# A three-block transformer kernel on one core: reordered steps in the convolution stage and in cross attention

## The chip, the core and the metric

The program runs on one core of a Trainium2 chip. The metric is the device time of one execution in microseconds (us); shown are the median of three runs and one profiled execution. TensorE is called PE here, VectorE DVE, ScalarE ACT, GpSimd POOL and SyncE SP, as in the profile.

## What is computed

512 tokens of width 1024 in float32 go through a first network (two layers of mixer, MLP and gated embedding) and then a second block, to which the change is confined:

```python
def second_block(x, mem, positions, ...):
    h = h + hybrid_mixer(rmsnorm(h), ...)      # w_in, w_out
    h = h + cross_attention(rmsnorm(h), rmsnorm(mem), w_cq, w_ckv, w_co)
    h = h + conv_ffn(rmsnorm(h), w_up, ffn_dw_w, w_down)
    return rmsnorm(h)

def hybrid_mixer(...):
    # q, k, v: 4 heads; q and k in two halves of 64, partly rotated
    a = softmax(q0 k0) - lam * softmax(q1 k1)     # causal, per head
    a = rmsnorm(a @ v) * 0.8
    c = u1 * sigmoid(u2)
    c = silu(layernorm(causal_dwconv(c, 31 taps)))   # 512 channels
    return concat(a, c) @ w_out

def cross_attention(h, m, ...):
    # 4 heads of 256, 256 memory tokens
    p = softmax(q @ k / 16);  return (p @ v) @ w_co
```

## The kernel before, in words

Activations lie features first: 8 tiles of 128 features by 512 tokens. Every product in float32 is made of three passes of a reduced format: a tensor is split into a high part (`aH`, written by ACT) and the rest (`aL`, written by DVE), weights likewise (`wH`, `wL`), and PE sums high by high, low by high and high by low (lines 468 to 470). One `linear` is 8 feature tiles times 3 passes, 24 matmuls of 512 columns.

**Weights.** SP copies pieces of 128x512 numbers in the order of `PLAN` into 4 buffers `raw`; POOL splits each into one of 7 pairs `wH`, `wL` (lines 2557 and 2559), and may write a pair only when PE has released the piece 7 back. A linear consumes 2 pieces. `open3` (plan) and `three_open`, `three_step` (PE) run three linears side by side, one feature tile after the other.

**Order.** Nothing schedules: each engine has its own function (`pe`, `act`, `dve`, `pool`, `sync`) in which the work is written in the order of issue, and an engine waits in that order for events of the others (`wait_ge`, `then_inc`). PE takes PSUM banks from a queue of 8 with `take`; `give(b, V, "rL", j)` puts a bank back and names the event that frees it, so a later, unrelated step can wait for that event.

**Convolution stage** (w_in to w_out). For each of the 4 heads of differential attention: `rotary_in(j)` is the linear of queries or keys, ACT copies it to `tmp[j % 2]`, `rotate(j)` is one PE permutation of `tmp`, three DVE steps turn it and `rotated(j)` splits it into `d_qH`, `d_qL`, `d_kH`, `d_kL`. `d_scores(hd)` are the scores in four row blocks n (line 978), with softmax by DVE (maxima, line 2359) and ACT (exponentials, line 1206). `d_turned(hd)` transposes the probabilities (line 1007) and splits them into `uH`, `uL`. `d_values(hd)` multiplies by the values. `stat_end("dn", hd)` sums the squares (line 501), ACT makes the root (`rstd`), `d_normed(hd)` normalizes and splits. The convolution's 31 taps run on DVE for three groups of 128 channels (`some_taps`) and on PE for the fourth, as diagonal matrices that ACT makes (`diagonals`, `conv_taps`, line 996). The layer norm takes its mean by PE ("mu", line 1051), squares on ACT, their sum on DVE and PE. `memory_keys` and `xvalues(half)` are keys and values of the memory for cross attention.

**Cross attention.** `stat_end("z")` and `columns("z")` turn the norm of the queries into a column; `x_head_in(hd)` are the two linears of a head's queries, `x_scores`, `x_turned` (line 1114), `x_values` the attention, and eight linears of `w_co` follow. `stat_end("f")` sums the squares for the next norm.

The lines that set the order in the convolution stage, on PE:

```python
for hd in range(2):
    d_turned(hd)
    d_scores(hd + 1, {1: conv_taps, 2: rotary_in(2 * hd + 4)})
    rotary_in(2 * hd + 5)
    rotate(2 * hd + 4); rotate(2 * hd + 5)
    conv_taps(20 + 8 * hd, min(24 + 8 * hd, 31))
    d_values(hd)
    stat_end("dn", hd, tiles=1, tail=False)
```

Of the kernel before, what the change touches and what calls it, by code (L numbers as in the profile page):

```python
# [37 lines left out]
def plan():  # L38
# [121 lines left out]
    for o in range(8):  # L160
        tile8("w_co_2", 0, 128 * o)
# [118 lines left out]
BY_PE = 3  # L280


def build(nc, xT, pT, memT, pos, pos2, vec, cst, ws, out):
    PLAN, BEHIND, DIVIDED = plan()
    with ExitStack() as ctx:
# [147 lines left out]
        def pe():  # L433
# [3 lines left out]
            def take(*event):  # L437
# [106 lines left out]
            def three_step(lin, k, xH, xL, ready, first=0, last=7, only=None):  # L544
                ws_, bs, events = lin
                for i in range(3):
                    if only in (None, i):
# [3 lines left out]
                        j = three(bs[i].ap[:, :], H, L, xH[:, k, :], xL[:, k, :], k == first, k == last)  # L551
# [406 lines left out]
            def rotate(j):  # L958
                b = take("rts", j)
# [51 lines left out]
            def d_values(hd):  # L1011
# [9 lines left out]
                give(b, V, "y2L", hd)  # L1021
# [17 lines left out]
            for hd in range(2):  # L1039
# [52 lines left out]
            def x_head_in(hd):  # L1092
                for d in range(2):
                    linear(("xq", hd, d), (V, "xqL", hd, d), "w_cq_2", 0, 128 * (2 * hd + d), aH, aL, z_ready)
# [36 lines left out]
            x_head_in(0)  # L1131
            x_scores(0)
            for hd in range(4):
                if hd < 3:
                    x_head_in(hd + 1)
                else:
                    P.also("z done")
                x_turned(hd)
                if hd < 3:
                    x_scores(hd + 1)  # L1140
                x_values(hd)
            P.also("x heads done")
            for o in range(8):
                w = block("w_co_2", 0, K8, ((128 * o, 128),))
                b = take("co", o)
                for k, (H, L, c, end) in enumerate(w):
                    P.wait_ge(G, "w", c)
                    P.wait_ge(V, "xoL", k // 2, k % 2)
# [6 lines left out]
            stat_end("f")  # L1155
            P.also("end cross")
            P.wait_ge(A, "end cross")
            P.wait_ge(V, "end cross")
# [23 lines left out]
        def root(*sid):  # L1182

            if sid[0] in ("mix", "mlp", "ple", "hs", "cq", "ckv", "ln"):
                return bk("stat", *sid)[:, :]
            return tab[1][0][:, 0:256] if sid == ("mem",) else rs[:, :]
# [3 lines left out]
        def act():  # L1190
# [397 lines left out]
            def rotary_in(j):  # L1588
                A.wait_ge(P, "rt", j)
                if j > 1:  # L1590
# [9 lines left out]
            def d_scores(hd):  # L1600
# [5 lines left out]
                for n in range(4):  # L1606
# [9 lines left out]
                    if n:  # L1616
                        divide(n - 1)
                divide(3)
# [13 lines left out]
            def d_normed(hd):  # L1632
                A.wait_ge(V, "dn", hd)
                do(uH[:, hd, :], bk("do", hd)[:, :], ACT.Copy).then_inc(*A.did("y2H", hd))
# [23 lines left out]
            d_scores(0)  # L1658
            diagonals(12, 16)
            rotary_in(2)  # L1660
# [4 lines left out]
            for hd in range(2):  # L1665
                d_turned(hd)
                d_scores(hd + 1)
                diagonals(20 + 8 * hd, 28 + 8 * hd)
                rotary_in(2 * hd + 4)
# [6 lines left out]
            convolved(2)  # L1676
            for i in range(4):
# [1016 lines left out]
```

## Time and profile before

| what | value |
|---|---|
| median of 3 runs (lowest, highest) | 2405.92 us (2403.82, 2407.05) |
| profiled execution, its own time | 2401.89 us |
| its span, first to last instruction | 2400.0 us |
| PE busy | 2298.3 us, 96% |
| POOL busy | 1563.6 us, 65% |
| DVE busy | 1269.0 us, 53% |
| ACT busy | 648.8 us, 27% |
| mean granted TensorE clock | 0.988 |

The profile counts an engine busy from the start of an instruction to its end; PE's ends are modelled and overlap the next start. Times in rows of the trace are us from the start of the span. The granted clock is 1.00 at 2.4 GHz and 0.50 at 1.2 GHz. The convolution stage ends near 1862 us; cross attention runs from there to 2028 us.

### The profile page before, as it was taken

To read this page: it belongs to the slowest core of one execution; us is meant where nothing else is said; L and a number is where in the kernel's file an instruction comes from. 1 tells how busy PE (TensorE), PEld (TensorE's weight loads), DVE (VectorE), ACT (ScalarE), POOL (GpSimd) and SP (SyncE) were. 2 spreads that over 40 slices of the span, in tenths; PEclk is the share of its full clock that TensorE was granted. 3 is DMA by queue.
4 is the path that set the end of the run, shared out by engine and by line. 5 is a ranking of instruction groups with operands and counts; after the bars stand their busy time and mean duration, and the time that the engine had idled before them with its cause. 6 is when DMAs were issued, how large, how long until landed. Compare 5 with 4: busy or idle time off the path is not lost.

```text
span 2400.0 us, 27442 instructions
## 1 busy us (share of the span) xinstructions
PE 2298.3 (96%) x10372; PEld 1860.2 (78%) x10372; DVE 1269.0 (53%) x1820; ACT 648.8 (27%) x1190; POOL 1563.6 (65%) x1530
## 2 busy tenths in 40 slices
PE   8999989999998899999999999999988999999998
PEld 6888877888887577778778888778647787888886
DVE  6674726235346666165454364468763443635444
ACT  3443432101014355154221011141444232202112
POOL 7556557877775454554597777598315946878784
PEclk9999999999999899999999999999998999999999
DMA  5222222333332111211233333233112422333332
GB/s 163 77 71 82 68 80 83 107 99 98 97 92 75 53 39 37 70 40 45 75 117 105 99 110 101 79 101 106 48 31 71 113 63 79 97 98 96 99 95 75
DMA packets 110867, 200.13 MB, mean 83 GB/s; under 512 B 12304, under 2 KB 18704, under 8 KB 110736
## 3 DMA queue, kind: packets, MB, share of 16 engines
q1 hardware_dynamic: 107568, 194.72, 27.0%
q10 hardware_dynamic: 3168, 3.67, 0.5%
q8 instruction: 82, 1.34, 0.2%
q14 instruction: 49, 0.40, 0.0%
HBM read 196.24 MB, written 2.10 MB: 83 GB/s over the span
## 4 chain that ended last, share of the span: by engine, by line
PE 87%; DVE 7%; ACT 2%; POOL 2%; issue 1%; DMA 0%; SPq 0%; DVEq 0%; POOLq 0%; ACTq 0%
PE bank L468 26%; PE bank L470 26%; PE bank L469 26%; DVE bank L1801 2%; DVE h L1793 1%; POOL wL L2559 1%; PE bank L501 1%; PE bank L996 1%; POOL wH L2557 1%; PE bank L862 1%; PE bank L867 1%; PE bank L868 1%; PE bank L863 1%; PE bank L864 1%; DVE aL L1801 1%
## 5 line engine op out<-in xcount | busy, mean ns | idle before, releaser
L2559 POOL TENSOR_TENSOR wL<-raw,wH 128x512 fp32r<-128x512 f32 (+2 forms) x731 | 997.9, 1365 | 60.9
L2557 POOL TENSOR_SCALAR wH<-raw 128x512 fp32r<-128x512 f32 (+2 forms) x731 | 528.9, 724 | 650.3 <-PE bank L470 558.4
L468 PE MATMUL bank<-aH,wH 128*128 128x512 f32 x1376 | 546.1, 397 | 18.1 <-DVE aL L1801 8.8
L470 PE MATMUL bank<-aH,wL 128*128 128x512 f32 x1376 | 537.6, 391 | 0.0
L469 PE MATMUL bank<-aL,wH 128*128 128x512 f32 x1376 | 537.1, 390 | 0.0
L468 PE MATMUL bank<-uH,wH 128*128 128x512 f32 x960 | 375.5, 391 | 5.6 <-DVE uL L1793 5.6
L469 PE MATMUL bank<-uL,wH 128*128 128x512 f32 x960 | 374.4, 390 | 0.0
L470 PE MATMUL bank<-uH,wL 128*128 128x512 f32 x960 | 374.3, 390 | 0.0
L468 PEld LDWEIGHTS bank<-aH,wH 128*128 128x128 f32 x1376 | 258.8, 188 | 77.8 <-issue 12.4
L469 PEld LDWEIGHTS bank<-aL,wH 128*128 128x128 f32 x1376 | 259.0, 188 | 56.3 <-issue 3.7
L470 PEld LDWEIGHTS bank<-aH,wL 128*128 128x128 f32 x1376 | 258.7, 188 | 54.9
L468 PEld LDWEIGHTS bank<-uH,wH 128*128 128x128 f32 x960 | 180.8, 188 | 44.6 <-ACT uH L1205 6.4
L469 PEld LDWEIGHTS bank<-uL,wH 128*128 128x128 f32 x960 | 180.8, 188 | 37.9 <-issue 0.5
L470 PEld LDWEIGHTS bank<-uH,wL 128*128 128x128 f32 x960 | 180.7, 188 | 37.8
L1205 ACT ACTIVATE uH<-mr 128x512 fp32r<-128x512 f32 x64 | 40.5, 633 | 391.0 <-DVE mr L1801 391.0
L1793 DVE TENSOR_TENSOR F<-F,bank 128x512 f32<-128x512 f32 x56 | 38.5, 687 | 190.0 <-PE bank L470 190.0
L1801 DVE SCALAR_TENSOR_TENSOR mr<-bank,rs 128x512 f32<-128x512 f32 x64 | 44.0, 688 | 157.9 <-PE bank L470 142.0
L1801 DVE SCALAR_TENSOR_TENSOR bank<-F,vs,bank 128x512 f32<-128x512 f32 x138 | 103.8, 752 | 34.9 <-ACT bank L1205 23.8
L1793 DVE TENSOR_TENSOR h<-h,bank 128x512 f32<-128x512 f32 x88 | 60.4, 686 | 112.4 <-PE bank L470 110.8
L1793 DVE TENSOR_TENSOR sums<-sums,sq 128x512 f32<-128x512 f32 (+1 forms) x72 | 78.3, 1088 | 76.5 <-ACT sq L1205 76.4
L2566 POOL TENSOR_SCALAR m_P<-m_P,m_stat 128x512 f32<-128x512 f32 x64 | 44.7, 698 | 102.0 <-DVE m_stat L2217 100.0
L1801 DVE SCALAR_TENSOR_TENSOR c_cb<-c_xb,vs,c_cb 128x511 f32<-128x511 f32 x88 | 82.4, 937 | 40.3 <-ACT c_cb L1205 38.7
(306 smaller groups left out, 3209.7 us busy)
## 6 DMA issues: line engine op xcount, KB each, us to landing
raw<-in_ws SPq DMA_DIRECT2D x699, 256.0 KB, 2.6
raw<-in_ws SPq DMA_DIRECT2D x24, 192.0 KB, 2.3
h<-in_xT SPq DMA_DIRECT2D x4, 512.0 KB, 6.6
E<-in_memT ACTq DMA_DIRECT2D x16, 128.0 KB, 2.5
out<-c_F SPq DMA_DIRECT2D x8, 256.0 KB, 2.1
tmp<-in_pT ACTq DMA_DIRECT2D x4, 256.0 KB, 3.6
raw<-in_ws SPq DMA_DIRECT2D x8, 128.0 KB, 2.0
g_hc<-in_cst SPq DMA_DIRECT2D x1, 640.0 KB, 9.2
```

Of the source, the lines that this page charges most:

```text
L468: P.e.matmul(o, lH, rH, start=start, stop=False, skip_group_check=skip)
L469: P.e.matmul(o, lH, rL, start=False, stop=False, skip_group_check=skip)
L470: return P.e.matmul(o, lL, rH, start=False, stop=stop, skip_group_check=skip)
L501: i = P.e.matmul(b.ap[:, 0:n], ones, sums[:, 0:n], start=True, stop=not tail)
L862: P.e.matmul(b.ap[:, :], m_qnH[:, c], m_knH[:, :], start=True, stop=False)
L863: P.e.matmul(b.ap[:, :], m_qnH[:, c], m_knL[:, :], start=False, stop=False)
L1205: return A.e.activation(o, i, func, bias=bias, scale=scale)
L1793: return V.e.tensor_tensor(o, a, b, op)
L1801: return V.e.scalar_tensor_tensor(o, a, s, b, op0, op1)
L2557: G.e.tensor_scalar(H, x, 1.0, 0.0, MUL, ADD).then_inc(*G.did("wH", n))
L2559: G.e.tensor_tensor(L, x, H.bitcast(F32), SUB).then_inc(*G.did("w", n))
L2566: G.e.tensor_scalar(x, x, m_st[:, 4 * (hd % 2) + n, 2:3], 0.0, MUL, ADD).then_inc(*G.did("mP", hd, n))
```

## The change

PE, ACT and DVE are given another order from the first rotated head to the first linear of the last feed-forward. No multiplication is added or removed; a DVE sum of four squares is written as a tree, and three results get another place (`tmp[0]` for the normalized head, `C` for the layer norm's root, `C` and `Sn` for squares). `order` lists instructions as they are issued. Names: `tmp` the copied projection, `F` the diagonals and probabilities, `cs` constants, `d_VH` values, `x_kH` memory keys; line numbers of the changed kernel are larger.

PE, head 1 of the convolution stage, from the last matmul of its second projection (before; the values follow both permutations and the taps):

```order
L470 MATMUL bank<-aH,wL 128x512
L961 MATMUL bank<-tmp,cs 128x512 x2
L996 MATMUL bank<-F,sq 128x512 x4
L468 MATMUL bank<-uH,d_VH 128x512
L469 MATMUL bank<-uL,d_VH 128x512
```

and from the last matmul of the values to the next scores:

```order
L470 MATMUL bank<-uH,d_VL 128x128
L501 MATMUL bank<-sums,cs 128x512
L1007 MATMUL bank<-cs,F 128x128 x10
L978 MATMUL bank<-d_kH,d_qH 128x128 x2
L978 MATMUL bank<-d_kL,d_qH 128x128 x2
```

The changed order at the same two places:

```order
L471 MATMUL bank<-aH,wL 128x512
L963 MATMUL bank<-tmp,cs 128x512
L469 MATMUL bank<-uH,d_VH 128x512
L470 MATMUL bank<-uL,d_VH 128x512
L471 MATMUL bank<-uH,d_VL 128x512
```

```order
L471 MATMUL bank<-uH,d_VL 128x128
L963 MATMUL bank<-tmp,cs 128x512
L998 MATMUL bank<-F,sq 128x512 x3
L502 MATMUL bank<-sums,cs 128x512
L998 MATMUL bank<-F,sq 128x512
L1009 MATMUL bank<-cs,F 128x128 x10
```

The values now stand between the two permutations, and the second permutation and three taps between the values and the sum of squares, one tap behind it.

ACT at the end of the first head's softmax, before:

```order
L1206 ACTIVATE bank,d_stat<-bank,d_stat 128x512 [waits dve_tile_written]
L1205 ACTIVATE F<-F,d_stat 128x384 [waits dve_tile_written]
L1205 ACTIVATE F<-F,d_stat 128x512 [waits dve_tile_written]
L1205 ACTIVATE sq<-cs,vs 128x128 [waits pe_group_done] x4
L1205 ACTIVATE tmp<-bank 128x512 [waits pe_group_done] x2
```

and in the change:

```order
L1230 ACTIVATE F<-F,d_stat 128x256 [waits dve_tile_written]
L1230 ACTIVATE sq<-cs,vs 128x128 [waits pe_group_done] x4
L1230 ACTIVATE tmp<-bank 128x512 [waits pe_group_done]
L1231 ACTIVATE F,d_stat<-bank,d_stat 128x512 [waits dve_tile_written]
L1231 ACTIVATE bank,d_stat<-bank,d_stat 128x512 [waits dve_tile_written]
L1230 ACTIVATE F<-F,d_stat 128x384 [waits dve_tile_written]
L1230 ACTIVATE F<-F,d_stat 128x512 [waits dve_tile_written]
```

The four diagonals and the first copy to `tmp` moved ahead of the last row block's exponentials.

PE in cross attention around the transposes of a head, before:

```order
L469 MATMUL bank<-aL,wH 128x512
L470 MATMUL bank<-aH,wL 128x512
L1114 MATMUL bank<-cs,F 128x128 x8
L468 MATMUL bank<-x_kH,uH 128x256
L469 MATMUL bank<-x_kL,uH 128x256
```

and in the change:

```order
L470 MATMUL bank<-aL,wH 128x512
L471 MATMUL bank<-aH,wL 128x512
L1120 MATMUL bank<-cs,F 128x128 x8
L469 MATMUL bank<-aH,wH 128x512
L470 MATMUL bank<-aL,wH 128x512
```

One of the two query linears now stands behind the transposes, ahead of the next scores. The diff, cut to its core:

```diff
@@ plan
-    for o in range(8):
+    open3(*[("w_co_2", 0, 128 * o) for o in range(3)])
+    for o in range(3, 8):
         tile8("w_co_2", 0, 128 * o)
@@ pe: take, rotate, d_values
-                b = banks.pop(0)
+                b = banks.pop(1 if second else 0)
...
-                give(b, V, "y2L", hd)
+                give(b, V, "dn", hd)
@@ pe: heads 0 and 1 of the convolution stage
-                rotate(2 * hd + 5)
-                conv_taps(20 + 8 * hd, min(24 + 8 * hd, 31))
                 d_values(hd)
+                rotate(2 * hd + 5, second=True)
+                conv_taps(20 + 8 * hd, 23 + 8 * hd)
                 stat_end("dn", hd, tiles=1, tail=False)
+                if hd == 0:
+                    conv_taps(23, 24)
+            d_turned(2)
             b = take("mu")
...
-            d_turned(2)
             d_scores(3, {1: lambda: memory_keys(4)})
             memory_keys(6)
-            stat_end("ln", tiles=4, tail=False, freed=(V, "lnn", 3))
+            b = take("stat", "ln")
+            P.wait_ge(V, "sum", ("ln",))
+            P.e.matmul(b.ap[:, :], ones, sq[:, :], start=True, stop=True).then_inc(*P.did("stat", "ln"))
+            give(b, A, "ln", "ln")
             d_values(2)
+            d_turned(3)
             stat_end("dn", 2, tiles=1, tail=False)
-            d_turned(3)
             xvalues(0)
             d_values(3)
-            stat_end("dn", 3, tiles=1, tail=False)
...
                 three_step(lin, k, uH, uL, y2_ready, last=3)
+                if k == 0:
+                    stat_end("dn", 3, tiles=1, tail=False)
@@ pe: cross attention
-            stat_end("z")
             xvalues(1)
-            columns("z")
+            stat_end("z")
...
+            def co_step(*ks):
+                for k in ks:
+                    three_step(lin, k, None, None, co_ready, tiles=x_o)
...
-            x_head_in(0)
+            x_head_in(0, 0)
+            columns("z")
+            x_head_in(0, 1)
+            x_head_in(1, 0)
             x_scores(0)
             for hd in range(4):
                 if hd < 3:
-                    x_head_in(hd + 1)
+                    x_head_in(hd + 1, 1)
+                x_turned(hd)
+                if hd < 2:
+                    x_head_in(hd + 2, 0)
+                elif hd == 2:
+                    lin = three_open([("w_co_2", 0, 128 * o) for o in range(3)], [("co", o) for o in range(3)])
+                    co_step(0)
                 else:
-                x_turned(hd)
+                    co_step(2, 3)
                 if hd < 3:
                     x_scores(hd + 1)
+                if hd == 2:
+                    co_step(1)
                 x_values(hd)
-            for o in range(8):
+            co_step(4, 5, 6, 7)
+            for o in range(3, 8):
...
-            stat_end("f")
...
                         linear(("cu", tile, j), ...)
+                        if tile == 0 and j == 0:
+                            stat_end("f")
@@ act
-            diagonals(12, 16)
-            rotary_in(2)
+            d_scores(0, {2: lambda: (diagonals(12, 16), rotary_in(2))})
...
+                d_scores(hd + 1, {2: lambda: (convolved(2) if hd else None, diagonals(20 + 8 * hd, 28 + 8 * hd), rotary_in(2 * hd + 4))})
                 rotary_in(2 * hd + 5)
                 rotate(2 * hd + 4)
+                d_values(hd)
                 rotate(2 * hd + 5)
-                d_values(hd)
                 rstd(128, "dn", hd)
+                d_turned(hd + 1)
                 d_normed(hd)
...
+            d_scores(3, {1: squares})
             memory_keys(4)
             memory_keys(6)
+            d_values(2)
             rstd(512, "ln")
+            d_turned(3)
             rstd(128, "dn", 2)
...
+            xvalues(1)
             rstd(1024, "z")
@@ dve
+            d_scores(0, {2: lambda: some_taps(4)})
+            turned_by_cos(2)
             rotate(2)
+            turned_by_cos(3)
             rotate(3)
...
+                d_scores(hd + 1, {2: lambda: some_taps(4)} if hd == 0 else {1: lambda: some_taps(200)})
+                turned_by_cos(2 * hd + 4)
+                some_taps(1)
                 rotate(2 * hd + 4)
+                turned_by_cos(2 * hd + 5)
+                rotated(2 * hd + 4)
                 rotate(2 * hd + 5)
                 rotated(2 * hd + 5)
                 d_normed(hd)
+                d_turned(hd + 1)
```

`turned_by_cos` is the first of the three DVE steps of a rotation, now issued by itself; `between` runs a function after row block n. `d_normed` writes `tmp[0]`, so its bank is freed by the first step of the norm ("dn") and no longer by the last ("y2L").

## Rows read from the trace of the kernel before

**Rows 1.** The page, part 1: busy us, share of the span, instructions.

```profile
PE 2298.3 (96%) x10372; PEld 1860.2 (78%) x10372; DVE 1269.0 (53%) x1820; ACT 648.8 (27%) x1190; POOL 1563.6 (65%) x1530
```

**Rows 2.** Windows: stretch, length, busy PE, PEld, DVE, ACT, POOL, granted clock, DMA.

```profile
1762.00:1766.00 4.00, 4.00 (x8) 1.70 (x8) 3.17 (x8) 2.06 (x9) 0.00 (x0) 0.57 0.02 4
...
1799.00:1807.00 8.00, 4.96 (x25) 4.96 (x26) 4.77 (x13) 4.21 (x15) 1.78 (x2) 0.57 0.01 3
...
1827.00:1834.00 7.00, 5.14 (x13) 4.07 (x14) 3.36 (x7) 3.52 (x5) 1.90 (x2) 0.51 0.01 2
...
1905.00:2030.00 125.00, 119.26 (x573) 97.85 (x573) 53.86 (x115) 35.26 (x75) 71.14 (x73) 1.00 0.27 80
```

**Rows 3.** PE's waits, 1717 to 1863 us: for whom, us in total, times, longest.

```profile
PE bank L468 <- DVE F L1801: 5.2, 1, 5.2
PE bank L978 <- DVE uL L1793: 3.3, 3, 2.6
PE bank L468 <- DVE uL L1793: 3.1, 1, 3.1
PE bank L501 <- ACT sums L1205: 2.9, 4, 0.8
PE bank L961 <- ACT tmp L1205: 2.3, 3, 1.7
PE bank L468 <- DVE d_qL L1793: 2.2, 2, 1.6
PE bank L1051 <- ACT F L1205: 1.6, 1, 1.6
PE bank L978 <- DVE F L1801: 0.6, 1, 0.6
```

**Rows 4.** PE's waits, 1863 to 2035 us.

```profile
PE bank L468 <- DVE uL L1793: 4.5, 5, 1.4
PE bank L504 <- ACT sq L1205: 2.4, 2, 1.2
```

**Rows 5.** Timeline of PE at the z norm: start, us, instruction, idle before.

```profile
1889.45 0.40 PE L470 MATMUL bank<-uH,wL 128*128 128x512 f32 x1
1889.68 1.02 PE L501 MATMUL bank<-sums,cs 128*128 128x512 f32 x2
```

**Rows 6.** Timeline of PE, a matmul of `xvalues(0)` at the lower clock.

```profile
1831.56 0.63 PE L468 MATMUL bank<-wH,x_mH 128*128 128x512 f32 x1
```

**Rows 7.** Timelines of PE, ACT and DVE from head 0's sum of squares.

```profile
1755.27 1.13 PE L501 MATMUL bank<-sums,cs 128*128 128x512 f32 x2 [0.69 <-ACT sums L1205]
1756.23 1.25 PE L1007 MATMUL bank<-cs,F 128*128 128x128 f32 x10
...
1761.21 0.39 PE L978 MATMUL bank<-d_kH,d_qH 64*128 64x256 f32 x2 [0.23 <-DVE uL L1793]
...
1758.61 1.91 ACT L1205 ACTIVATE uH<-bank 128x512 fp32r<-128x512 f32 x5 [0.83 <-DVE bank L1801]
...
1757.82 0.76 DVE L1801 SCALAR_TENSOR_TENSOR bank<-bank,lam,rs 128x512 f32<-128x512 f32 x1 [4.16 <-ACT rs L1205]
1759.31 2.28 DVE L1793 TENSOR_TENSOR uL<-bank,uH 128x512 fp32r<-128x512 f32 x5 [0.73 <-ACT uH L1205]
```

**Rows 8.** Timelines of POOL and DVE before and in `xvalues(1)`.

```profile
1886.00 1.82 POOL L2559 TENSOR_TENSOR wL<-raw,wH 128x512 fp32r<-128x512 f32 x1
...
1897.20 1.30 POOL L2559 TENSOR_TENSOR wL<-raw,wH 128x512 fp32r<-128x512 f32 x1
...
1899.16 1.29 POOL L2559 TENSOR_TENSOR wL<-raw,wH 128x512 fp32r<-128x512 f32 x1
...
1886.59 1.78 DVE L1793 TENSOR_TENSOR sums<-sums,sq 128x512 f32<-128x512 f32 x1
```

**Rows 9.** Timelines: first scores of cross attention (PE), last division (DVE).

```profile
1917.73 0.39 PE L468 MATMUL bank<-x_kH,uH 128*128 128x256 f32 x1 [1.41 <-DVE uL L1793]
...
1923.69 0.81 DVE L1797 TENSOR_SCALAR F<-F,x_stat 128x256 f32<-128x256 f32 x1
```

More of the change, by code:

```diff
@@ L435, in pe, with take @@
             at = 0
-            def take(*event):
-                b = banks.pop(0)
+            def take(*event, second=False):
+                b = banks.pop(1 if second else 0)
                 if b.freed:
@@ L542, in three_done, with three_step @@
                     j.then_inc(*P.did("w", lin[0][i][k][2]))
-            def three_step(lin, k, xH, xL, ready, first=0, last=7, only=None):
+            def three_step(lin, k, xH, xL, ready, first=0, last=7, only=None, tiles=None):
                 ws_, bs, events = lin
@@ L550, in three_step @@
                         ready(k)
-                        j = three(bs[i].ap[:, :], H, L, xH[:, k, :], xL[:, k, :], k == first, k == last)
+                        x = tiles[k] if tiles else (xH[:, k, :], xL[:, k, :])
+                        j = three(bs[i].ap[:, :], H, L, *x, k == first, k == last)
                         three_done(lin, i, k, j, last)
@@ L956, in rotary_in, with rotate @@
                 linear(("rt", j), (V, "rL", j), "w_in_2", 0, (512 if j % 2 else 0) + 128 * (j // 2), aH, aL, n1_ready)
-            def rotate(j):
-                b = take("rts", j)
+            def rotate(j, second=False):
+                b = take("rts", j, second=second)
                 P.wait_ge(A, "rt", j)
@@ L1086, in pe, with x_head_in @@
             P.also("y2 done")
[L1087 removed]
             xvalues(1)
             P.also("mem done")
[L1090 to L1094 removed]
+            stat_end("z")
+            def x_head_in(hd, d):
+                linear(("xq", hd, d), (V, "xqL", hd, d), "w_cq_2", 0, 128 * (2 * hd + d), aH, aL, z_ready)
             def x_scores(hd):
@@ L1617, in d_scores @@
                         divide(n - 1)
+                    if n in between:
+                        between[n]()
                 divide(3)
@@ L1633, in d_normed @@
                 A.wait_ge(V, "dn", hd)
-                do(uH[:, hd, :], bk("do", hd)[:, :], ACT.Copy).then_inc(*A.did("y2H", hd))
+                do(uH[:, hd, :], tmp[0][:, :], ACT.Copy).then_inc(*A.did("y2H", hd))
             def convolved(i):
@@ L1718, in act, with x_head_in @@
             A.wait_ge(P, "y2 done")
+            xvalues(1)
             rstd(1024, "z")
-            xvalues(1)
-            def x_head_in(hd):
-                for d in range(2):
-                    A.wait_ge(P, "xq", hd, d)
-                    if hd > 1:
-                        A.wait_ge(P, "xs", hd - 2, 3)
-                    do(x_qH[hd % 2][:, d, :], bk("xq", hd, d)[:, :], ACT.Copy).then_inc(*A.did("xqH", hd, d))
+            def x_head_in(hd, d):
+                A.wait_ge(P, "xq", hd, d)
+                if hd > 1:
+                    A.wait_ge(P, "xs", hd - 2, 3)
+                do(x_qH[hd % 2][:, d, :], bk("xq", hd, d)[:, :], ACT.Copy).then_inc(*A.did("xqH", hd, d))
             def x_scores(hd):
@@ L2363, in d_scores @@
                         combine(n - 1)
+                    if n in between:
+                        between[n]()
                 combine(3)
@@ L2372, in d_normed @@
             def d_normed(hd):
-                y = bk("do", hd)[:, :]
+                y = tmp[0][:, :]
                 V.wait_ge(A, "rstd", "dn", hd)
-                stt(y, y, lam[:, 5:6], root("dn", hd), MUL, MUL).then_inc(*V.did("dn", hd))
+                V.wait_ge(V, *(("rr", 2 * hd + 4) if hd < 2 else ("y2L", hd - 1)))
+                stt(y, bk("do", hd)[:, :], lam[:, 5:6], root("dn", hd), MUL, MUL).then_inc(*V.did("dn", hd))
                 V.wait_ge(V, "dn", hd)
@@ L2419, in dve, with add_ln_squares @@
                 stt(d_acc[:, i, :], bk("mu")[:, :], -1.0 / 512, d_acc[:, i, :], MUL, ADD).then_inc(*V.did("cent", i))
-            for i in range(1, 4):
-                add_squares(("ln",), i)
-            d_turned(2)
-            d_scores(3)
+            def add_ln_squares():
+                x = (sq, tmp[1], C, Sn)
+                for i in (0, 2):
+                    V.wait_ge(A, "sq", ("ln",), i + 1)
+                    tt(x[i][:, :], x[i][:, :], x[i + 1][:, :], ADD).then_inc(*V.did("sum2", ("ln",), i))
+                V.wait_ge(V, "sum2", ("ln",), 2)
+                tt(sq[:, :], sq[:, :], C[:, :], ADD).then_inc(*V.did("sum", ("ln",)))
+            d_scores(3, {1: add_ln_squares})
             memory_keys(4)
             memory_keys(6)
-            d_normed(2)
             V.wait_ge(A, "rstd", "ln")
@@ L2457, in dve, with x_head_in @@
             residual("z", "wo", ("z",), lambda k: vv("norm_cross_g_2", k))
+            def x_head_in(hd, d):
+                V.wait_ge(A, "xqH", hd, d)
+                low(x_qL[hd % 2][:, d, :], bk("xq", hd, d)[:, :], x_qH[hd % 2][:, d, :]).then_inc(*V.did("xqL", hd, d))
             xvalues(1)
+            x_head_in(0, 0)
             column(x_rc[:, 0, :], "z")
@@ L2462, in dve @@
             ts(x_rc[:, 2, :], x_rc[:, 0, :], -1.0 / 16, None, MUL, None).then_inc(*V.did("xrc"))
-            def x_head_in(hd):
-                for d in range(2):
-                    V.wait_ge(A, "xqH", hd, d)
-                    low(x_qL[hd % 2][:, d, :], bk("xq", hd, d)[:, :], x_qH[hd % 2][:, d, :]).then_inc(*V.did("xqL", hd, d))
             def x_scores(hd):
```

81 lines of the change are left out of this document (41 added, 40 removed).

## The prediction

> **What bounds the kernel now.** I read the page's line of busy engines first [rows 1]: PE is busy 2298.3 us of a span of 2400.0, the next engine, POOL, 65%. PE works in the order in which its instructions are written, so the time is PE's work plus PE's waits plus what the clock takes. Then came the view of waits, for PE alone, over the two stages that the change touches. In the convolution stage PE waits 21.2 us in 16 waits [rows 3], in cross attention 6.9 us in 7 [rows 4]; together 28.1 us in 23. Then the timelines around each wait, to find the step that ends late and what stands next on PE. Last the windows with the granted clock [rows 2]: three stretches, of 4, 8 and 7 us, show 0.57, 0.57 and 0.51, which is 1.2 GHz nearly throughout, while the stretch of 125 us in cross attention shows 1.00. In all three, PE had waited several times between short matmuls before the clock fell.
>
> A wait costs more than its idle time. A matmul that follows another at once starts 0.23 us behind it, one that follows a wait needs 0.40 us from start to end [rows 5]: about 0.16 us of refill for each wait.
>
> PE's work does not change: the diff moves matmuls and removes none. The gain can come from three places only: idle time, refill, clock. I add them up, and then look at what the moved steps hide behind.
>
> **The change, part by part.**
>
> *The waits of the convolution stage.* The largest, 5.2 us, is the first matmul of `xvalues(0)`, which waits for a bank that the layer norm's last scaling frees. Its new place follows values, transposes and the sum of squares, and the norm starts earlier: it goes. The 3.1 us (a `memory_keys` bank) and the 2.2 us of the values' bank were waits for lows that an unrelated step releases; another place in the queue of banks or an earlier release ("dn" in place of "y2L") removes them. The 2.9 us in 4 before the sums of squares are DVE and ACT turning the values into squares with nothing on PE meanwhile; now a permutation and taps or another head's transposes stand there, each about 1 us. The 2.3 us in 3 before the permutation (line 961) vanish since the copy to `tmp` is issued by ACT ahead of the last exponentials and the second permutation stands behind the values. The 1.6 us before the mean have the transposes of head 2 in front.
>
> What stays, or is new, I work out one by one:
> - (a) The 0.6 us before the scores that depends on DVE's probabilities: nothing near it moves. 0.5 us.
> - (b) Head 0's last group of transposes now needs the bank that the norm's first step frees. Before, from the start of the sum of squares to the end of that step took 1757.82 + 0.76 − 1755.27 = 3.3 us [rows 7]. PE has meanwhile the sum of squares (0.96 us, from 1755.27 to 1756.23), a tap of the same form (taken as 0.96 too) and nine of the ten transposes (1.0 of 1.25 us, less the refill): 2.9 us. 0.4 to 0.5 remain.
> - (c) The next scores, row block 1, need a bank freed by the lows of the transposed probabilities. These now stand behind the norm: 3.3 us to the norm, one ACT step more in between (estimated at 0.6, from five uH copies of mixed width in 1.91 us), 0.7 to the first lows, and 1.9 from these to the scores (1759.31 to 1761.21, [rows 7]): 6.5 us from the start of the sum. PE is there at 3.4 + 0.9 = 4.4. A wait of 2.1 us, in place of the 2.6 of [rows 3].
> - (d) Head 1 as (b), but with no tap behind its sum: 3.3 − 1.9 = 1.4 us.
> - (e) Some short waits of the transposes of head 3 for banks, 0.3 us together.
>
> Together 4.8 us of 21.2 in the convolution stage.
>
> *Cross attention.* The three waits of about 0.6 us and the one of 1.4 us in [rows 4] were values behind transposes whose lows were not yet there; a whole linear (24 matmuls of 0.23, 5.5 us) or a step of three output linears (2.1 us) stands between now. They go; (g) that of the last head, about 1.2 us, stays. The 2.4 us of the two sums of squares go: the first now stands behind `xvalues(1)`, the second behind the first linear of the next stage. But `xvalues(1)` then starts at 1889.7 where the sum stood [rows 5] and no longer behind it and its wait, and eats pieces faster than POOL makes them: 6 matmuls, 1.4 us a piece, against 1.96 us for a pair (1897.20 to 1899.16, from low part to low part [rows 8]). Its eighth piece is wanted at 1889.7 + 7 × 1.4 = 1899.5 and ready at 1899.16 + 1.29 = 1900.45: (f) a wait of 1.0 us.
>
> Is the softmax still covered, with one linear of queries there where two stood? In [rows 9] the last division ends at 1923.69 + 0.81 = 1924.5, 6.8 us after the first of the scores. Scores are 24 matmuls of half the columns, 2.9 us, and the linear is 5.5: 8.4 us. It is, with 1.6 us to spare. Were it not, each head would pay the lack at once, on PE.
>
> Sum of the waits: 28.1 − 4.8 − 1.0 − 1.2 = 21.1 us gone. Some ten waits remain of 23; 13 × 0.16 = 2.1 us of refill.
>
> *Clock.* A granted clock of 0.57 means 0.50 for 86% of the stretch. PE was busy in the three stretches 4.00, 4.96 and 5.14 us [rows 2], of which at the lower level about 3.4 + 4.3 + 5.1 = 12.8 us, and a matmul of 512 columns took 0.63 us there [rows 6] against 0.40. Half of this busy time is the loss, 6.4 us. The longest waits of the pattern go, but (b) with (c), and (d), are still waits among small matmuls, so I keep two stretches of the kind of the first, 3.4 us each, PE busy throughout: 3.4 us of loss. Gain 3.0. The ends are no gain (or a loss of 3, if each of the two lasts as long as the second did) and 6.4.
>
> *At nothing.* DVE's and ACT's instructions keep their number and engines at 53% and 27% [rows 1]; the moved taps and diagonals go where these engines waited (DVE 4.16 us ahead of the norm's step [rows 7]). If that cover were gone, the norm chain of (b) to (d) would grow by as much. Three output linears opened early hold six weight pairs of the 7 at most for a step of 2.1 us each; POOL then has its work later, not more. The step of the residual, three tiles at once, is caught up by the fifth output tile.
>
> **Sum.** 21.1 + 2.1 + 3.0 = 26.2 us against the profiled execution's 2401.89, which lies 4.0 under the median of the runs; the same difference from the median gives 2405.9 − 26.2 = **2379.7 us**.
>
> **The rivals.**
>
> *The clock stays low as long as before.* For it: the waits (b) to (d) still alternate with short matmuls, as in [rows 2]. Against: the summed idle time in that stage falls to a quarter. The time: gain 23.2, 2382.7 us. Chance 0.15. By the Trainium skill, TensorE: Matmul & The Clock Gate, section "A second HAM failure mode: psum-queue depth-cycling", short idle times between groups of matmuls are enough to make the clock swing, so on that page's rule alone this rival would be the forecast; the trace agrees that the clock fell among such waits.
>
> *POOL becomes the bound in `xvalues(1)`.* With DVE's sum of 1.78 us beside it, the low part took 1.82 instead of 1.29 [rows 8]. If the pairs came every 2.4 us in the place of 1.96, the wait (f) would be 1.0 + 8 × 0.4 = 4 to 5 us: 2384 us. Chance 0.08. The Trainium skill, GPSIMD Engine Reference, section "1. Specifications", has GpSimd's SBUF interfaces shared with VectorE, with contention where a DVE instruction has two SBUF inputs; both long rows are of that kind.
>
> *New waits behind the moved steps take half.* Each bank freed by an earlier event puts a later, unrelated step behind it; (b), (c) and (d) could be 3 us each if ACT or DVE, with the steps of the softmax interleaved, comes to the norm later than before. Then half of the gain remains: 2393 us. Chance 0.12.
>
> *Slower: the clock falls in cross attention.* There it is 1.00 over 125 us, because long linears stand between the groups of short matmuls; the change leaves one linear where two stood. If it fell there, a microsecond of work at half the clock costs another: from 26 us of full-speed work done at 1.2 GHz, a fifth of that stretch, the whole gain is lost; with three fifths of it, 75 us, the sum is 2379.7 + 75 = 2455 us. Against: the waits there shrink too, to 2.2 us. Chance 0.03.
>
> *No difference.* The rest, 0.02: the order on PE does change, as its listing shows, so this needs two mishaps at once.
>
> **The numbers.** The forecast as worked out has 0.60. Its own bounds: if (b) to (f) all vanish, 5 us better, and with the whole clock back 3.4 more, 2371; if (f) is 4, (c) and (d) twice as long and the clock gives nothing, 10 worse, 2390. Both at their ends is unlikely. The range that holds 8 in 10 is 2373 to 2391.5; outside lie most of "half is taken" and the slow case, and the best corner. A measurement of this kernel tells 0.2%, 4.8 us, from no change: faster 0.94, same 0.03 and slower 0.03, since every case but the last two is faster by 12 us or more.
>
> **What would show it.** In the profile after, PE's busy time should lie 3 us lower or so, and its waits between the heads' first rotation and the output projection should sum to about 5 us, not 21, with none above 2.5; no wait at the first matmul of `xvalues(0)` or at the permutations; in cross attention one of about 1.2 in the last values, and one of about 1 in `xvalues(1)` that names POOL's wL. The windows should show at most two short stretches near 0.5, and 1.00 through the heads of cross attention. Wrong I would be if waits for the norm's banks, "dn" or the low parts, stand there with several us each, if POOL's wait in `xvalues(1)` is over 3, or if the clock falls in a new place.

## The result

The changed kernel took 2371.48 us (median of 4 runs, 2370.67 to 2372.49), the kernel before 2406.34 us beside it (4 runs, 2403.82 to 2407.05): ratio 0.9857, 95% interval 0.984 to 0.9874, 34.9 us faster. The forecast was 2379.7 us, 26.2 us faster, with a range down to 2373: the direction was right and the gain a quarter too small, 1.5 us outside the range.

| what | before | after |
|---|---|---|
| profiled execution, its own time | 2401.89 us | 2372.49 us |
| its span | 2400.0 us | 2370.6 us |
| PE's waits, convolution stage | 21.2 us in 16 | 4.2 us in 4 |
| PE's waits, cross attention | 6.9 us in 7 | 0.6 us in 2 |
| stretches near 1.2 GHz in the changed part | 3 | none |

The page of the changed kernel, part 1, in the order of [rows 1]:

```profile
PE 2291.2 (97%) x10372; PEld 1857.8 (78%) x10372; DVE 1271.2 (54%) x1820; ACT 648.5 (27%) x1190; POOL 1568.0 (66%) x1530
```

The numbers of instructions are those of before, on every engine: nothing was added or left out. PE is 7 us less busy for the same 10372 matmuls, which is the clock and the refills of all stages together.

PE's waits of the changed kernel, 1717 to 1842 us, to be read against [rows 3] (engine, tile, line, releaser: us in total, times, longest):

```profile
PE bank L980 <- DVE uL L1826: 2.6, 2, 2.0
PE bank L1009 <- DVE tmp L1834: 1.6, 2, 1.2
```

and 1842 to 2010 us, against [rows 4]:

```profile
PE bank L469 <- POOL wL L2612: 0.6, 2, 0.3
```

Seven of the eight groups of [rows 3] have vanished. What is left are the scores behind the lows of the transposed probabilities (0.6 and 2.0) and, new, the transposes behind the norm's first step (0.4 and 1.2), both of which the prediction named. In cross attention only POOL's weights in `xvalues(1)` are waited for.

Windows of the changed kernel (stretch, length, busy PE, PEld, DVE, ACT, POOL, granted clock, DMA), against [rows 2]:

```profile
1754.00:1764.00 10.00, 7.62 (x38) 4.24 (x38) 7.27 (x17) 5.54 (x16) 0.00 (x0) 1.00 0.01 2
1784.00:1790.00 6.00, 4.76 (x19) 2.40 (x17) 3.37 (x7) 3.25 (x7) 0.00 (x0) 1.00 0.00 1
1795.00:1842.00 47.00, 47.00 (x254) 39.17 (x254) 21.80 (x38) 23.38 (x45) 34.18 (x34) 1.00 0.30 90
1842.00:2010.00 168.00, 167.40 (x788) 137.19 (x787) 79.31 (x139) 47.30 (x95) 119.55 (x116) 1.00 0.31 91
```

The first two hold the waits that remain, and the clock stays at 2.4 GHz through both. Where before three stretches of 19 us in all lay mostly at 1.2 GHz, none does.

**The changed part by itself.** The two kernels issue the same PE instructions up to the last group of eight taps ahead of the change (the row `L996 MATMUL bank<-F ... x8`, L998 in the changed kernel), and again at the end. So one window from that row to 339 us before the last instruction holds the same 1526 matmuls in every kernel of this document. Before, and in the change:

```profile
1700.34:2060.95 360.61, 332.30 (x1526) 256.44 (x1526) 179.85 (x333) 122.30 (x269) 191.53 (x190) 0.98 0.23 69
1704.15:2031.59 327.44, 322.61 (x1526) 252.12 (x1526) 183.18 (x333) 121.99 (x269) 196.41 (x190) 1.00 0.26 76
```

The changed part is 33.2 us shorter: PE is busy for 9.7 us less and idle for 23.5 us less. The whole profiled executions differ by 29.4 us only, because the 7404 matmuls ahead of this window, the same in both kernels, are done by 1700.3 us in one execution and by 1704.2 in the other.

### The profile page after: what moved, and what is told of

The parts are those of the page before. It is cut to its first block, busy times and chain, and to the rows that moved or that the text cites. A ratio compares the mean times of both kernels' runs of the same rounds, so it can differ in the third digit from the quotient of the medians.

```text
span 2370.6 us, 27451 instructions
## 1 busy us (share of the span) xinstructions
PE 2291.2 (97%) x10372; PEld 1857.8 (78%) x10372; DVE 1271.2 (54%) x1820; ACT 648.5 (27%) x1190; POOL 1568.0 (66%) x1530
## 4 chain that ended last, share of the span: by engine, by line
PE 87%; DVE 6%; POOL 4%; ACT 2%; issue 1%; DMA 0%; SPq 0%; DVEq 0%; POOLq 0%
PE bank L469 26%; PE bank L471 25%; PE bank L470 25%; POOL wL L2612 2%; POOL wH L2610 1%; DVE bank L1834 1%; DVE h L1826 1%; PE bank L998 1%; PE bank L502 1%; PE bank L864 1%; DVE tmp L1826 1%; PE bank L869 1%; PE bank L870 1%; PE bank L865 1%; PE bank L866 1%
```

## The experiments

**How much do runs of the kernel before differ, and why?** The forecast was made against one execution, which was 4 us quicker than the median of the other runs. The kernel before was therefore run as it is, as an experiment of its own (no edit); its profiled execution is called the usual one below.

> The kernel before, nothing changed, for the spread of its own runs. The profiled execution that the forecast was made against took 2401.9 us, its other runs 2403.8 to 2407.1. Theory A (the low clock stretches differ from run to run): the runs spread over 3 us or more, and the longer ones show a mean granted clock that is lower by about 0.001 for each 2 to 3 us. Theory B (the profiled execution was just better for another reason): the clocks are equal and the runs still differ.

It took 2406.48 us (10 runs, 2404.79 to 2408.44), ratio 1.0 (0.999 to 1.0009), and none of these or of the 17 runs beside it was as quick as 2401.89. Of 13 more runs of it, taken later beside other experiments, three were (2401.86, 2402.14 and 2402.19), each with a mean clock of 0.987. In the first set, the runs up to 2405 us show a mean clock of 0.986 and those over 2406.9 one of 0.985. Its profiled execution took 2405.45 us with 0.987, so the mean alone does not order single runs. Its windows:

```profile
1762.00:1770.00 8.00, 7.80 (x24) 3.95 (x20) 4.91 (x14) 2.40 (x11) 0.00 (x0) 0.57 0.01 2
1804.00:1811.00 7.00, 5.94 (x30) 5.94 (x31) 3.79 (x12) 3.00 (x13) 2.26 (x3) 0.55 0.00 1
1831.00:1838.00 7.00, 5.79 (x15) 4.57 (x16) 2.71 (x6) 2.86 (x5) 2.06 (x3) 0.53 0.01 2
1612.00:1616.00 4.00, 3.54 (x9) 2.81 (x10) 3.97 (x5) 2.49 (x4) 3.83 (x5) 0.57 0.26 76
```

and the last of these windows in the execution that the forecast read:

```profile
1612.00:1616.00 4.00, 3.66 (x16) 3.05 (x17) 3.93 (x6) 2.37 (x4) 3.83 (x5) 1.00 0.22 71
```

This is theory A. The stretch behind head 0's norm lasts 3.4 us in one execution (from 1762.1 us, [rows 2]) and 6.8 in the other (from 1762.5), and there is one near 1612 us, in a stage that the change does not touch, which the first execution did not have. Worked as in the prediction (low share times busy PE, halved), the three stretches of the changed part cost 3.35 + 2.67 + 2.72 = 8.7 us here against 6.4 there. The waits are equal in both to 0.1 us. The changed part by itself:

```profile
1701.98:2064.51 362.53, 334.29 (x1526) 257.93 (x1526) 179.33 (x333) 122.26 (x269) 191.29 (x190) 0.97 0.24 69
```

That is 1.9 us longer than in the execution of the forecast and 35.1 us longer than in the change. Another 1.6 us lie ahead of it, in work that no kernel here alters. Over all 14 profiled executions that work ends between 1700.3 and 1704.6 us, so differences below 4 us are better read from the changed part than from whole times.

**The two parts of the change by themselves.** First the convolution stage's part alone: its hunks of the diff, with the plan, the PE, ACT and DVE order of cross attention left as before.

```diff
+                give(b, V, "dn", hd)
+                rotate(2 * hd + 5, second=True)
+            give(b, A, "ln", "ln")
...
             stat_end("z")
             xvalues(1)
             columns("z")
```

> The convolution stage's part of the change alone, cross attention as before. Theory A (waits, refill and the whole clock loss of the stage come back): waits 21.2 to 4.2 us, 17.0 gone; 11 waits fewer, 1.9 of refill; 6.4 of clock: 25 us faster, ratio 0.9895. Rival (the clock recovers only where cross attention is changed too): 19 us, ratio 0.992, and stretches near 0.5 in the trace.

Measured 2377.8 us against 2406.13, ratio 0.9884 (0.9869 to 0.9899): 28.3 us, more than the 25 expected. One window over the heads of this kernel, 1754 to 1842 us:

```profile
1754.00:1842.00 88.00, 84.38 (x437) 64.62 (x436) 48.44 (x95) 42.51 (x96) 42.89 (x43) 1.00 0.20 60
```

The clock comes back with this part alone, and at the prices of the usual execution, 17.0 of waits, 1.9 of refill and 8.7 of clock, the sum is 27.6. The changed part says the same: 334.9 us, 27.6 less than in the usual execution. The rival falls. Then cross attention's part alone:

```diff
-            stat_end("z")
             xvalues(1)
-            columns("z")
+            stat_end("z")
...
+                    x_head_in(hd + 1, 1)
+                x_turned(hd)
+                if hd < 2:
+                    x_head_in(hd + 2, 0)
```

> Cross attention's part of the change alone. Theory A: 6.9 us of waits become 0.6, with 5 refills 7 us faster, ratio 0.997, the convolution stage with its three low stretches as before. Rival (the two parts help each other, so each alone gives less): under 5 us.

Measured 2398.79 us, ratio 0.9968 (0.9957 to 0.9978), 7.3 us: as expected (7.5 us in the changed part, against the usual execution). The three low stretches of the convolution stage are all there. The two parts give 28.3 + 7.3 = 35.6, the whole 34.9; they do not need each other.

**Is the last head's wait hidden by the two steps of w_co?** The prediction left 1.2 us there.

```diff
-                else:
-                    co_step(2, 3)
...
-            co_step(4, 5, 6, 7)
+            co_step(2, 3, 4, 5, 6, 7)
```

> The changed kernel with the steps 2 and 3 of the output projection behind the last head's values instead of between its transposes and its values. The forecast left a wait of 1.2 us there and the changed kernel shows none. Theory A (these two steps are what hides it): the 1.2 us come back, with the refill 1.4 us slower than the change. Rival (it is hidden by something earlier, such as lows that are ready sooner): no wait, no difference.

The time, 2372.42 us, ratio 0.9859 (0.9844 to 0.9873), cannot show 1.4 us; the waits of cross attention do:

```profile
PE bank L469 <- DVE uL L1824: 1.2, 1, 1.2
PE bank L469 <- POOL wL L2610: 0.6, 2, 0.3
```

The 1.2 us is back, and the changed part takes 1.4 us longer than in the change, as theory A has it. In the change these steps lie between the transposes and the values, and the prediction overlooked that.

**The sum z ahead of xvalues(1) again.**

```diff
+            stat_end("z")
             xvalues(1)
             P.also("mem done")
-            stat_end("z")
```

(on ACT `rstd(1024, "z")` likewise.)

> The changed kernel with the sum of squares z ahead of xvalues(1) again, on PE and on ACT. Theory A: its wait of 1.2 us returns and POOL's two waits of 0.3 us in xvalues(1) go, since it starts later; net 0.6 us slower, which three rounds can hardly tell, but the waits in the trace can. Rival (POOL's waits stay, since they come from its own pace): 1.4 us slower.

2373.01 us, ratio 0.9867 (0.985 to 0.9883), inside the spread of the change's own runs (2370.67 to 2373.6). The whole list of waits in its cross attention is

```profile
PE bank L505 <- ACT sq L1230: 1.2, 1, 1.2
```

so POOL's waits are gone and the sum's own is back: the move trades 1.2 us for 0.6, and no more. The changed part is 0.3 us longer. POOL's waits come from the earlier start, as the prediction had it.

**What makes the clock fall?** In the changed kernel ACT repeats one step of the norm's root, so that the waits behind it grow and nothing else changes. Twice:

```diff
+                A.wait_ge(P, "stat", "dn", hd)
+                for i in range(2):
+                    do(rs[:, :], bk("stat", "dn", hd)[:, :], ACT.Ln, bias=eps, scale=1.0 / 128).then_inc(*A.did("again", hd, i))
+                    A.wait_ge(A, "again", hd, i)
                 rstd(128, "dn", hd)
```

> The changed kernel with ACT repeating the logarithm of the norm's root twice in heads 0 and 1 (same numbers, nothing else changed), so that the norm comes later by about 1.4 us. The waits behind it (0.4 and 2.0 in head 0, 1.2 in head 1) then grow by 1.4 in each head: 2.8 us. Theory A (the clock falls once PE stands still longer among short matmuls; the kernel before fell behind a wait of 2.6 us): at about 3.8 us in head 0 and 2.6 in head 1 one low stretch comes back, cost 1.7 to 3 us, total 5 to 6 us slower than the change, ratio to before 0.988. Rival (the falls came from the whole row of waits in the kernel before): no stretch below 0.95 near 1755 to 1800 us, 3 us slower, ratio 0.987.

Measured 2377.4 us, ratio 0.988 (0.9864 to 0.9897), 5.9 us slower than the change. Its waits and windows:

```profile
PE bank L1009 <- DVE tmp L1838: 4.5, 2, 2.7
PE bank L980 <- DVE uL L1830: 2.6, 2, 2.0
```

```profile
1758.00:1764.00 6.00, 4.83 (x14) 2.70 (x15) 5.93 (x16) 2.23 (x9) 0.00 (x0) 0.72 0.01 3
1789.00:1794.00 5.00, 4.55 (x8) 2.01 (x9) 2.69 (x6) 1.55 (x5) 0.00 (x0) 0.66 0.01 2
```

Waits of 1.8 and 2.0 us in head 0 and a single one of 2.7 in head 1 each have a low stretch of 3.4 us behind them. The waits cost 7.1 − 4.2 = 2.9 us, the two stretches by their windows 1.4 + 1.5 = 2.9. The changed part took 6.2 us longer. The ratio alone would fit the rival too; the stretches decide. Four times:

```diff
+                for i in range(4):
```

> As the one with two, with four repeats: the norm 2.8 us later, waits 5.6 us longer in sum. Theory A: low stretches in both heads, 4 to 6 us of clock besides, 10 to 12 us slower than the change, ratio to before 0.990. Rival: 6 us slower, clock 1.00, ratio 0.988.

2381.07 us, ratio 0.9895 (0.988 to 0.9909), 9.6 us slower than the change: the waits grew by 5.2 us (3.3 and 1.4 in head 0, 4.1 in head 1, 9.4 in sum), the stretch in head 0 is three times as long,

```profile
1756.00:1768.00 12.00, 9.02 (x25) 4.79 (x25) 8.89 (x19) 4.88 (x16) 0.00 (x0) 0.57 0.00 1
1793.00:1798.00 5.00, 4.35 (x7) 1.89 (x8) 2.88 (x6) 1.74 (x5) 0.00 (x0) 0.66 0.01 2
```

and costs some 3.9 us, the one in head 1 1.5; the changed part took 10.3 us longer. Both runs fit theory A: the idle time added in this place is paid about twice.

The same from the other side, the kernel before with its longest wait taken out:

```diff
-            stat_end("ln", tiles=4, tail=False, freed=(V, "lnn", 3))
+            stat_end("ln", tiles=4, tail=False)
...
-            if sid[0] in ("mix", "mlp", "ple", "hs", "cq", "ckv", "ln"):
+            if sid[0] in ("mix", "mlp", "ple", "hs", "cq", "ckv"):
...
+            return tab[1][0][:, 0:256] if sid == ("mem",) else C[:, :] if sid == ("ln",) else rs[:, :]
```

> The kernel before with one wait taken out: the layer norm's root is written to C (as the change does), so that its bank is free as soon as ACT has read it and the first matmul of xvalues(0) no longer waits 5.2 us for the last scaling. Theory A (a long wait is paid twice, as idle time and by the low clock behind it): the stretch of 7 us at 0.51 behind it goes too, 5.2 + 0.2 + 2.6 = 8 us faster, ratio 0.9967. Rival (the clock there answers to the many short waits before it and stays low): 5.4 us, ratio 0.9978, and the stretch stands at the same place.

2399.45 us against 2405.14, ratio 0.9972 (0.9963 to 0.9982): 5.7 us by the medians, with an interval of 4 to 9 us that holds both expectations. The windows decide it:

```profile
1763.00:1772.00 9.00, 8.10 (x24) 4.26 (x24) 5.93 (x15) 3.42 (x13) 0.00 (x0) 0.62 0.01 2
1805.00:1813.00 8.00, 5.95 (x30) 5.95 (x31) 4.08 (x13) 3.94 (x14) 2.27 (x3) 0.57 0.00 1
1820.00:1860.00 40.00, 38.45 (x189) 31.49 (x188) 17.84 (x27) 19.42 (x34) 25.03 (x25) 1.00 0.30 85
```

The first two stretches stand, the third is gone with the wait of 5.2 us, though the shorter waits ahead of it are all there (the wait of 0.8 us before a sum of squares among them). So the third stretch belongs to the long wait and not to the short ones. Whole times do not show 8 us, but the changed part does: it is 7.9 us shorter than in the usual execution, whose first two stretches are as long as here. The wide interval comes from the runs: two of the ten took 2395 us, at a mean clock of 0.989, the others 2398 to 2400.

**Where exactly does the clock fall?** Before, the second and the third stretch begin while PE still stands in a wait:

```profile
1802.04 0.58 PE L468 MATMUL bank<-x_mH,wH 128*128 128x256 f32 x1 [3.05 <-DVE uL L1793]
1828.86 0.77 PE L468 MATMUL bank<-wH,x_mH 128*128 128x512 f32 x1 [5.24 <-DVE F L1801]
```

```profile
1799.70:1802.00 2.30, 0.00 (x0) 0.00 (x0) 1.60 (x4) 1.94 (x5) 0.00 (x0) 0.50 0.01 4
1823.70:1827.00 3.30, 0.00 (x0) 0.00 (x0) 2.32 (x4) 2.45 (x7) 0.00 (x0) 1.00 0.02 8
1827.00:1828.90 1.90, 0.04 (x1) 0.07 (x1) 1.90 (x4) 1.89 (x3) 0.00 (x0) 0.50 0.00 0
```

The third falls 3.3 us after its long wait began. The second falls 0.7 us after the wait of 3.1 us began, so what went before counts there: waits of 0.6, 0.7, 1.6 and 0.6 us in the 15 us ahead of it. The first falls at 1762.1, behind waits of 1.7, 1.6, 0.7, 2.6 and 0.2 us in 19 us. The second stretch can therefore not be put down to its long wait alone. Whether the wait of 2.6 us alone would have brought the first is open: no run here takes single waits out of these rows.

**Can the remaining waits be removed?** In head 0 of the changed kernel the squares are ready at 1750.3 us, while PE comes to their sum after three taps (timeline of PE: start, us, instruction, idle before):

```profile
1749.44 1.07 PE L963 MATMUL bank<-tmp,cs 128*128 128x512 f32 x2
1750.35 2.74 PE L998 MATMUL bank<-F,sq 128*128 128x512 f32 x6
1752.93 1.02 PE L502 MATMUL bank<-sums,cs 128*128 128x512 f32 x2
...
1756.18 0.33 PE L1009 MATMUL bank<-cs,F 128*128 128x128 f32 x1 [0.38 <-DVE tmp L1834]
...
1759.35 0.39 PE L980 MATMUL bank<-d_kH,d_qH 64*128 64x256 f32 x2 [1.99 <-DVE uL L1826]
```

```diff
-                conv_taps(20 + 8 * hd, 23 + 8 * hd)
+                conv_taps(20 + 8 * hd, 21 + 8 * hd)
                 stat_end("dn", hd, tiles=1, tail=False)
-                if hd == 0:
-                    conv_taps(23, 24)
+                conv_taps(21 + 8 * hd, min(24 + 8 * hd, 31))
...
-                if hd:
-                    V.wait_ge(P, "ctap")
-                    ts(d_acc[:, BY_PE, :], ...)
                 d_normed(hd)
+                if hd:
+                    V.wait_ge(P, "ctap")
+                    ts(d_acc[:, BY_PE, :], ...)
```

> The changed kernel with the sum of squares of heads 0 and 1 behind one tap of the convolution instead of three; the other taps follow it. The squares are ready at 1750.3 us, the sum starts only at 1752.9. If the norm's chain alone sets the waits of 0.4, 2.0 and 1.2 us behind it, they go, 3.6 us, with two or three refills: 4 us faster than the change, ratio to before 0.984. Rival (DVE gets to the norm's step no earlier, since the rotation's lows stand ahead of it): under 2 us.

2371.54 us, ratio 0.9856 (0.9841 to 0.9871): no gain, in the changed part neither (0.1 us). Its waits in the stage sum to 4.1 us, as against 4.2:

```profile
PE bank L980 <- DVE uL L1825: 3.1, 2, 2.5
PE bank L1009 <- DVE x_kL L1825: 0.8, 1, 0.8
PE bank L1055 <- DVE F L1829: 0.2, 1, 0.2
```

The waits for the norm's step are gone, and the one at the scores grew to 2.5. The size is the rival's, its reason is not: DVE starts the norm's step 1.1 us earlier (1754.26 us against 1755.37). Neither theory had what happened: ACT issues the norm's high part behind the four transposed copies, these wait for PE, and DVE has the norm's low part ahead of the lows that the scores need.

The run shows one thing more. Around this wait of 2.5 us, which has no other in the 27 us ahead of it, the clock stays at 1.00:

```profile
1754.00:1764.00 10.00, 7.53 (x37) 4.15 (x35) 7.02 (x17) 4.39 (x15) 0.00 (x0) 1.00 0.01 2
```

In all four profiled executions with the waits of before in heads 0 and 1 (the kernel before twice, cross attention's part alone, the longest wait taken out), the clock fell behind the wait of 2.6 us, which had three waits of 1.7, 1.6 and 0.7 us ahead of it. The lone wait of 2.7 us in head 1 of the kernel with two repeats had a fall behind it, however. These are one execution each, so what decides between a lone wait of 2.5 and one of 2.7 us stays open.

So one more edit, on ACT:

```diff
                 rstd(128, "dn", hd)
-                d_turned(hd + 1)
                 d_normed(hd)
+                d_turned(hd + 1)
```

> The early sum of squares again, and on ACT the norm's high part ahead of the next head's four transposed copies instead of behind them. In the first version the wait at the next scores became 2.5 us, since this copy stood behind copies that wait for PE. Theory A (the order on ACT and DVE sets that wait, no longer the norm): 2.5 becomes about 0.6, and with the other waits the kernel is 2 us faster than the change, ratio to before 0.985. Rival (the time reappears in head 3, whose transposes waited 0.8 us for the softmax in the first version): no difference from the change, the waits moved there.

2367.8 us, ratio 0.9838 (0.9824 to 0.9853): 3.7 us faster than the change, where 2 were expected. The wait at the scores is down to 0.6, and the 0.8 of head 3 is gone too, so the rival falls. Why head 3's wait went is not shown. The same kernel and the unaltered change were then run together, on another chip:

> The early sum of squares with the norm's high part ahead on ACT, once more with more rounds. Waits of 0.6 and 0.6 us in the convolution stage in place of 4.2: 3.7 us faster than the change, 2367.8 us. If it was luck of the clock in unchanged stages, under 2 us.

> The changed kernel, nothing altered, on the same chip as the version with the early sum of squares. 2371.5 us as before, ratio 0.9857, and no granted clock below 1.00 between 1650 us and the last stage's end.

The early version took 2367.35 us (2366.8 to 2367.91), ratio 0.9842 (0.9827 to 0.9857); the change 2373.46 us (2373.14 to 2373.6), ratio 0.9867 (0.9853 to 0.9882): 6.1 us between them, with no overlap of the runs. All that PE still waits in the stage is

```profile
PE bank L980 <- DVE uL L1825: 1.2, 2, 0.6
```

3.0 us less than in the change. In the changed part the early version is 3.5 us shorter than the first execution of the change, with the clock at 1.00 in both: waits and refill. The rest of the 6.1 is clock, for the second execution of the unaltered change did have a low stretch:

```profile
1757.00:1764.00 7.00, 6.84 (x15) 3.55 (x16) 6.39 (x16) 2.23 (x9) 0.00 (x0) 0.52 0.01 2
```

Its waits are to the tenth those of the other profiled execution, 2.6 and 1.6 us. The expectation of 1.00 was wrong here. Since the waits are equal, the two executions price one stretch of 6.8 us by themselves:

```profile
1701.97:2032.59 330.62, 325.80 (x1526) 253.53 (x1526) 183.55 (x333) 122.00 (x269) 196.51 (x190) 0.99 0.27 75
```

Against 327.44 us this is 3.2 us, all of it PE's busy time.

## Why the prediction was right in kind and too small

- **Bound and kind of gain: right.** PE bounds, its work is the same, and the time came from idle time, refill and clock. No rival with a new wait, nor the fall of the clock in cross attention, occurred.
- **The waits of the convolution stage: right within 0.6 us in sum.** Forecast 4.8 left, measured 4.2: (a) 0.6 for 0.5, though of the scores' two short waits it is the one for the lows that stayed and the one for the probabilities, which the prediction named, that went, (b) 0.4 for 0.4 to 0.5, (c) 2.0 for 2.1, (d) 1.2 for 1.4, (e) none for 0.3. For (c) the size was right, but the early sum of squares shows that the chain is not the norm alone: it also runs through ACT's copies behind PE's transposes.
- **Cross attention: 1.6 us too little.** The term (g) was wrong outright: the steps 2 and 3 of `w_co` hide the last head's wait of 1.2 us, as taking them away showed. (f) measured 0.6 for 1.0. With that 23.3 us of waits went, not 21.1, and 17 refills instead of 13, 2.7 us for 2.1.
- **The clock: the step that failed.** Two errors in the same term. "So I keep two stretches of the kind of the first" was an analogy with nothing measured behind it: 0.4 and 2.0 us of waits remain in head 0 and 1.2 in head 1, while two falls of before came with rows of waits up to 2.6 and 3.1 us, and the third with one of 5.2 us and without it not (the prediction put all three behind several waits), and in the profiled executions with the waits of the change (its own, the convolution part alone, the one with the two steps moved, the one with z moved, and the repeat) a stretch came back in one of five. And the 6.4 us of loss were read from one execution, which was quicker than all 27 runs of the first experiment; the next profiled one showed 8.7. The term was forecast at 3.0 and is 8.7 where no stretch remains: 3.4 us of the miss are the two stretches that did not stay, 2.3 the quick execution. That half of PE's busy time in a stretch is lost was right, though the 0.63 against 0.40 us that the prediction gives for it are not a factor of two; equal waits with and without a stretch show it, 3.2 us for a stretch with PE busy for 6.5.
- **The sum with these sizes:** 23.3 + 2.7 + 8.7 = 34.7 us, and the changed part measures 35.1 against the usual execution. With the 6.4 us of the quick execution it is 32.4, and the changed part measures 33.2 against that one. Of the 8.5 us between 26.2 and 34.7 the clock is 5.7, the waits 2.2 and the refill 0.6.
- **The two levels compared.** The prediction carried its difference over from a quick execution to the median, as if it were the same at both. It is not: of the 3.6 us by which the usual execution took longer, 1.9 lie in the changed part, mostly as clock that the change gives back, and 1.6 in work that it does not touch. How near the measured time came to the range is partly luck: the second measurement of the change gave 2373.46 us, 31.7 less than the kernel before beside it, with one low stretch in the profiled execution. The better end of the range, 2373, was too near by the same step: its best corner of 2371 needed all of the waits (b) to (f) gone besides the 6.4 us of clock.
- **The rival "the clock stays low"** fell. By the Trainium skill, TensorE: Matmul & The Clock Gate, "A second HAM failure mode: psum-queue depth-cycling", short idle times between groups suffice for the clock to swing. The trace agrees only in part: before, the clock fell at 1762.1 us behind five waits of 0.2 to 2.6 us, but with six waits of up to 2.0 us it stayed at 1.00 in the change's own execution, and the repeat had one low stretch.

## What to carry to other kernels

Price the waits of an in-order PE among short matmuls at their idle time plus the low stretch that goes with them. Look at all the waits ahead of each fall, and not only at the nearest: here 8.7 us of clock stood beside 21.2 us of waits, and a lone wait of 2.5 us had no stretch behind it. Read the clock's stretches in two executions before a sum is made, above all if the profiled one is quicker than the median. Compare kernels over the part that the change touches, from the same matmul to the same matmul: the untouched part alone varied by 4 us. When a chain to a waiting instruction is shortened, follow it on every engine: the early sum of squares gave nothing until ACT's order was changed with it.

## What the runs showed of the hardware that was not expected

- The same waits do not always give the same clock. After 0.4 and 2.0 us of waiting in head 0 it stayed at 1.00 in four profiled executions and fell to 0.52 over 7 us in a fifth; the stretch near 1612 us came and went between executions of one kernel. The length of a stretch varies as well: 3.4 us and 6.8 us behind the same wait of 2.6 us.
- Where waits were lengthened by 1.4 us in each head, the clock fell in both heads, in head 0 behind two waits of 1.8 and 2.0 us, in head 1 behind one of 2.7. A lone wait of 2.5 us in head 0 left it at 1.00 in the one execution that had it.
- A fall can come within a wait. The one of 1827.0 us came 3.3 us after the start of a wait of 5.2, and the one of 1799.7 us 0.7 us after the start of a wait of 3.1.
